# A Mamba-2 mixer's scan: the far outputs transposed back into PSUM first, the own blocks one slot later on top of them

## What is computed

```python
def ssd_chunked(x, dt, a_neg, bm, cm):            # one direction, chunks of 128 tokens
    def step(state, inp):
        cum = jnp.cumsum(ac, axis=1)
        decay = jnp.exp(jnp.where(mask, cum[:, :, None] - cum[:, None, :], -jnp.inf))
        scores = jnp.einsum('btgn,bsgn->btsg', cc, bc)
        y_intra = jnp.einsum('btsg,btsgr,bsgr,bsgrp->btgrp', scores, decay, dtc, xc)
        y_state = jnp.einsum('btgn,bgrpn,btgr->btgrp', cc, state, jnp.exp(cum))
        ...
        return state, y_intra + y_state

def mamba2_bidir_mixer(h, ...):
    proj = h @ w_in                                # gives z, x, B, C and dt
    ...
    y = y_fwd + y_bwd + d_skip[:, None] * xs
    u = (y * silu(z)); u = u * rsqrt(mean(u * u)) * norm_g   # by group
    return u @ w_out
```

## Time and profile before

| | |
|---|---|
| time, median of 3 runs | 2614.88 us (2612.96 to 2616.8) |
| span of the profiled execution | 2614.5 us, the one time that is listed for it |
| PE busy, share of the span | 2547.8 us, 97% |
| DVE busy | 2072.9 us, 79% |
| ACT busy | 1366.4 us, 52% |
| POOL busy | 662.4 us, 25% |
| DMA | 679.73 MB, mean 260 GB/s |
| mixer: first scores of a scan to the last | 1225 to 1860 us of the span |

### The profile page before, as it was taken

The page is one execution under the profiler, slowest core; times in us unless marked ns, Lnnn a source line. Parts: engine busy times, 40 slices in busy tenths (PEclk is TensorE's granted clock), DMA queues, the critical chain, the costliest instruction groups (busy, mean ns, idle before and its releaser), DMA issues.

```text
span 2614.5 us, 45356 instructions
## 1 busy us (share of the span) xinstructions
PE 2547.8 (97%) x15582; PEld 2257.1 (86%) x15582; DVE 2072.9 (79%) x2637; ACT 1366.4 (52%) x2149; POOL 662.4 (25%) x576
## 2 busy tenths in 40 slices
PE   7799999999999999999999999999999999999998
PEld 6799999888888888888788888888888888888887
DVE  7988888898888988758788898888899655555554
ACT  4544444544444444556666646766654444444454
POOL 0011122343444444320011042113333111111123
PEclk8999999999999999999999999999999999999999
DMA  9979988898988989746555598554479555555554
GB/s 395 416 291 368 370 335 304 277 359 306 334 332 328 320 334 326 262 165 204 186 194 194 194 350 286 194 195 160 161 277 336 190 186 188 190 192 184 189 184 142
DMA packets 163918, 679.73 MB, mean 260 GB/s; under 512 B 18720, under 2 KB 18976, under 8 KB 139072
## 3 DMA queue, kind: packets, MB, share of 16 engines
q1 hardware_dynamic: 163728, 677.75, 72.9%
q0 software_dynamic: 48, 0.13, 0.0%
HBM read 675.58 MB, written 2.23 MB: 259 GB/s over the span
## 4 chain that ended last, share of the span: by engine, by line
PE 81%; DVE 9%; issue 3%; DMA 3%; ACT 2%; POOL 0%; DVEq 0%; ACTq 0%; SPq 0%; POOLq 0%
PE psm L1155 43%; PE psm L1158 21%; DVE wl L1484 4%; PE psm L1233 3%; PE psm L1235 3%; PE psm L1234 3%; DVE adat L1497 2%; DMA xs<-in_ada 1%; PE psr L1193 1%; ACT wh L730 1%; PE psm L1449 1%; DVE xs L1497 1%; PE psr L1402 1%; DMA raw<-in_w 1%; PE psr L1449 1%
## 5 line engine op out<-in xcount | busy, mean ns | idle before, releaser
L1484 DVE TENSOR_TENSOR wl<-raw,wh 128x1024 fp32r<-128x1024 f32 x854 | 1109.1, 1300 | 357.4 <-ACT wh L730 354.8
L730 ACT ACTIVATE wh<-raw 128x1024 fp32r<-128x1024 f32 x854 | 897.8, 1053 | 310.1 <-DMA raw<-in_w 138.9
L1155 PE MATMUL psm<-hcat,wh 128*128 128x512 f32 x3120 | 986.6, 398 | 1.4 <-DVE pad L1795 1.4
L1155 PE MATMUL psm<-hid,wh 128*128 128x512 f32 x2240 | 704.6, 396 | 2.3 <-POOL hid L631 2.1
L1158 PEld LDWEIGHTS psm<-hcat,wl 128*128 128x128 f32 x3120 | 586.1, 188 | 138.6
L1158 PE MATMUL psm<-hcat,wl 128*128 128x256 f32 x3120 | 613.3, 278 | 0.0
L1158 PEld LDWEIGHTS psm<-hid,wl 128*128 128x128 f32 x2240 | 420.8, 188 | 99.3
L1155 PEld LDWEIGHTS psm<-hcat,wh 128*128 128x128 f32 x3120 | 476.1, 189 | 7.5 <-issue 5.2
L1497 DVE CUSTOM_DVE_ANT_0 adat<-adat,cond 128x2048 f32<-128x2048 f32 x176 | 434.7, 2470 | 15.8 <-DMA adat<-in_ada 15.7
L1158 PE MATMUL psm<-hid,wl 128*128 128x256 f32 x2240 | 440.1, 278 | 0.0
L1155 PEld LDWEIGHTS psm<-hid,wh 128*128 128x128 f32 x2240 | 341.3, 189 | 3.8 <-POOL hid L631 3.4
(11 more groups left out here) (257 smaller groups left out, 2640.1 us busy)
## 6 DMA issues: line engine op xcount, KB each, us to landing
raw<-in_w SPq DMA_DIRECT2D x866, 512.0 KB, 4.4
adat<-in_ada SPq DMA_DIRECT2D x176, 1024.0 KB, 6.9
dec<-running_sums SPq DMA_DIRECT2D x48, 256.0 KB, 5.9
xs<-in_ada SPq DMA_DIRECT2D x8, 1024.0 KB, 11.4
zs<-in_ada SPq DMA_DIRECT2D x8, 1024.0 KB, 11.6
normt<-running_sums SPq DMA_DIRECT2D x16, 256.0 KB, 4.9
x<-in_xT SPq DMA_DIRECT2D x4, 512.0 KB, 9.5
out<-x SPq DMA_DIRECT2D x4, 512.0 KB, 3.5
```

What stands on the lines that cost most here:

```text
L730: act.activation(wh[:, h % 4, :], raw[:, h % 4, :], ACT.Copy).then_inc(hi_done, 1)
L1155: pe.matmul(both, wh[:, h % 4, (k + i) * P:(k + i + 1) * P], src[:, kb + i, :, :], start=(kb + i == 0), stop=(kb + i == KB - 1), skip_grou ...
L1484: dve.tensor_tensor(wl[:, h % 4, :], raw[:, h % 4, :], wh[:, h % 4, :].bitcast(F32), ALU.subtract).then_inc(lo_done, 1)
```

## The change

On PE the eight products with the identity become eight transposes (`is_transpose`), and they come first: they open the sums in `psr` (`start`), and the own blocks are added on top. So the wait for `y_far` moves from the end of slot 6 to the start of slot 5. The own blocks of pieces 1 and 2 move from slot 4 to slot 5, piece 3 from slot 5 to slot 6; piece 4 stays in slot 6. (Group 0: far outputs and pieces 1 and 2 in slot 6, 3 and 4 in slot 7.) Within a piece the two heads alternate by chunk. The semaphore `y_back` goes; those that waited for it wait for `y_head`. As the pieces' buffers come free later, SP's loads of sums move to slots 5, 5, 6, 6 (group 0's scan: 6, 6, 7, 7), DVE's `segments` to 6, 7, 8, 9 (7, 8, 9, 9), and ACT's `decays` of pieces 1 and 2 to 7 and 8 (8 and 9).

```diff
+def segment_slots(g):
+
+    return {7: (1,), 8: (2,), 9: (3, 4)} if behind(g) else {6: (1,), 7: (2,), 8: (3,), 9: (4,)}
...
-                            if s == (0, 4 + behind(g - 1), 4 + behind(g - 1), 5 + behind(g - 1), 6)[piece]:
+                            if s == (5, 5, 6, 6)[piece - 1] + behind(g - 1):
                                 load_sums(g, piece)
...
-                    at_least(pool, y_back, g + 1)
+                    at_least(pool, y_head, g * HG + HG)
...
-                        for piece in {6: (1,), 7: (2,)}.get(s - behind(g - 1), ()):
+                        for piece in {7: (1,), 8: (2,)}.get(s - behind(g - 1), ()):
                             decays(g, piece)
...
+            def far_back(g):
+
+                at_least(pe, g_ready, g * 4 + 4)
+                at_least(pe, y_far, g * 2 + 4)
+                for b in range(XB):
+                    for ch in range(2):
+                        at = (b % 2) * T + ch * P
+                        pe.matmul(psr[b // 2][:, at:at + P], ytok[:, ch, b * P:(b + 1) * P], ident[:, :],
+                                  start=(b % 2 == 0 and ch == 0), stop=False, is_transpose=True,
+                                  skip_group_check=True)
+
             def own_block(g, piece):
 
                 at_least(pe, em_ready, g * 4 + piece)
                 b = piece - 1
-                for i in range(2):
-                    cols = slice((2 * b + i) * HD, (2 * b + i + 1) * HD)
-                    for ch in range(2):
-                        at = (b % 2) * T + ch * P
+                for ch in range(2):
+                    at = (b % 2) * T + ch * P
+                    for i in range(2):
+                        cols = slice((2 * b + i) * HD, (2 * b + i + 1) * HD)
                         mm = pe.matmul(psr[b // 2][i * HD:(i + 1) * HD, at:at + P], xd[:, 0, ch, cols],
                                        em[piece][:, 2 * ch + i, ch * P:(ch + 1) * P],
-                                       start=(b % 2 == 0 and ch == 0), stop=False,
-                                       skip_group_check=True)
-                    mm.then_inc(y_head, 1)
+                                       start=False, stop=(ch == 1 and b % 2 == 1), skip_group_check=True)
+                        if ch == 1:
+                            mm.then_inc(y_head, 1)
+                return mm
...
-                if s == 4 + behind(g):
-                    at_least(pe, g_ready, g * 4 + 4)
+                if s == 5 + behind(g):
+                    far_back(g)
                     for piece in (1, 2):
                         own_block(g, piece)
-                if s == 5 + behind(g):
-                    own_block(g, 3)
-                if s == 6:
-                    own_block(g, 4)
-                    at_least(pe, y_far, g * 2 + 4)
-                    for b in range(XB):
-                        for ch in range(2):
-                            at = (b % 2) * T + ch * P
-                            mm = pe.matmul(psr[b // 2][:, at:at + P], ytok[:, ch, b * P:(b + 1) * P], ident[:, :],
-                                           start=False, stop=True, skip_group_check=True)
-                    mm.then_inc(y_back, 1)
+                if s == 6 + behind(g):
+                    for piece in (3, 4):
+                        mm = own_block(g, piece)
...
-                    at_least(dve, y_back, g + 2)
+                    at_least(dve, y_head, g * HG + 2 * HG)
...
-                        for piece in {5: (1,), 6: (2,), 7: (3,), 8: (4,)}.get(s - behind(g - 1), ()):
+                        for piece in segment_slots(g - 1).get(s, ()):
                             segments(g, piece)
```

More of the change, by code:

```diff
@@ L314, in build @@
         em_ready, y_head = sem("em_ready"), sem("y_head")
-        y_back, v_done, vz_done, gsq = sem("y_back"), sem("v_done"), sem("vz_done"), sem("gsq")
+        v_done, vz_done, gsq = sem("v_done"), sem("vz_done"), sem("gsq")
         gss, gsum, grms, gu = sem("gss"), sem("gsum"), sem("grms"), sem("gu")
@@ L437, in build @@
         last = At(NG - 1)
-        AHEAD = [(y_head, HG), (y_far, 2), (y_back, 1), (v_done, XB), (grms, 1), (gu, XB), (u_lo, 1)]
+        AHEAD = [(y_head, HG), (y_far, 2), (v_done, XB), (grms, 1), (gu, XB), (u_lo, 1)]
         def first_slot(k):
```

## The result

The changed kernel takes **2662.68 us** (median of 4, 2661.34 to 2665.23) against 2615.73 us for the kernel before in the same sessions: ratio 1.0177, 95% interval 1.0165 to 1.0189. The forecast was 2655 us; it is slower by 47 us where 40 were worked out.

The account below looks back on a forecast made before the run. PE was taken as the bound, without gaps in an ordinary group. Waits 24.2, scan 0 -5.0, shift 9.0 and clock 11.9 sum to 40.1 us on 2614.5, plus 0.4 to the median: 2655 us, range 2632 to 2674.

Parts of the forecast that it names:

- The wait for `y_far`: PE at slot 5 stands for DVE's far product: +3.42 us per ordinary scan, 24.2 us over scans 1 to 7.
- The shift: Moved ACT and DVE steps make `y_far` 1.5 us later in scans 1, 2, 3, 5, 6, 7: 9.0 us.
- the meeting of DVE and POOL: In DVE's slot 9, piece 4 of `segments` brings work to meet POOL's 2.56 us product; 1.5 us charged.
- The clock: PE's granted clock falls behind the new gaps: 1.7 us in each of scans 1 to 7, 11.9 us.
- the wait alone: Rival: PE waits for `y_far` as in the old trace, shift hidden and clock held or recovered: 2634 us, chance 0.12.
- Scans 3 and 7: Scan 3, costed like the ordinary scans, was worked out 6.6 us longer; scan 7, over the output projection's slabs, 7.1.
- Scan 0: First scan gains, as PE's 4.29 us stand for piece 4 goes: -5.0 us, ends -2 and -5.7.
- PE's own cost: PE's scan work in slots 4 to 6 falls from 4.63 to 3.41 us: 1.22 us less per scan without waits.
- The rival of slow transposes: Rival: transposes with open sums take the products' 1.98 us, not 0.87: 8.9 us more, 2664 us, chance 0.07.
- The rival of heads that overlap only when they alternate: Rival: alternating heads halve own-block time once more on PE: 7.7 us less, 2647 us, chance 0.05.
- The other signs: In the new profile, the load of the root's table was to come 1.2 us later against its scan's scores.
- costing the DMAs at nothing: SP's moved loads of sums cost nothing; a late load would show as ACT waiting for `raw`.

Follow-up runs that it names:

- e1: The changed kernel with DVE's scaling of the far outputs (`y_far`) moved to right behind the first `wl` of its slot 3: 2621.61 us, ratio 1.0023.
- e4: The changed order of sums with transposes and all four own pieces in slot 6, the wait one slot later: 2619.2 us, ratio 1.0009.
- e2: The changed kernel with segments of piece 4 back in slot 8 and the exponential of piece 2 in the next group's slot 1: 2652.44 us.
- e3: The changed kernel with unused identity products on PE ahead of the `y_far` wait, 22 in scans 1, 2, 3, 5, 6 and 12 in scan 4: 2652.57 us.
- e7: The changed kernel with far outputs scaled earlier on DVE and the later steps of the decay pieces moved out of the way: 2607.19 us, ratio 0.9969.
- e5: The kernel before, with only its eight identity products made transposes, still last in slot 6 on top of the own blocks: 2609.37 us, ratio 0.9977.
- e6: The kernel before, with only the order within an own block changed, the two heads alternating by chunk: 2615.88 us, ratio 1.0001.
- e9: The kernel before with transposes last, scan 0's piece 4 and far outputs one slot later, own blocks in two visits, not three: 2602.56 us.
- e10: The kernel before with transposes last, scan 0's late steps one slot later, two own-block visits and heads alternating by chunk: 2600.38 us, ratio 0.9938.

## Why the prediction was right

**The wait for `y_far`.** The main step, that PE comes to slot 5 ahead of DVE's far product, held in every scan from 1 to 7 and not in scan 0. From the scores, the transposes start at 38.45 us where slot 5 had begun at 32.72. e1 takes the wait away by moving two DVE instructions, e4 by moving PE's step: both take back over 40 us. That DVE can't be sooner, as I wrote, holds only for its steps in the order as it stands: e1 changes that order, and `y_far` comes 4.6 us sooner.

**The shift.** Foreseen as 1.5 us a scan, measured as 2.14 in scans 2, 3, 5 and 6 and as nothing in scan 1 (38.3 before and after). The step that was mis-sized is the meeting of DVE and POOL: I charged 1.5 us for it, but piece 4 took 2.15 us longer (3.28 against 1.13). In scan 7 it was larger still (below). And the 1.5 us charged in scan 1 did not come at all, since there `y_far` already lay at 38.3 us before the change. The shift also stands behind a cost that I had left out: the gap of 1.57 us ahead of unit 4, which e2 removes in scans 2, 3, 5 and 6. In the changed kernel that gap costs little of its own, as PE would have spent it at slot 5.

**The clock.** 1.7 us a scan was a fair mean, and in part luck: e3 gives 1.9, 1.4, 2.7, 1.4, 2.7, together 10.0 where 8.5 were worked out, and scan 4, where I charged 1.7 for the 2.99 us gap, kept its clock. The rival *the wait alone*, 2634 us, is refuted by e2 and e3 at once: shift and clock cost 10 us each.

**Scans 3 and 7** lost 3.1 and 2.5 us more than worked out. In scan 3, 1.0 is clock, and 1.2 lies in the output units behind it, where PE stands 1.08 us for `wl`. That gap is in the traces of the changed kernel, e1 and e3, and only 0.20 us of it in e2 and e7, which take the later steps of the pieces away; so the moved steps of ACT and DVE bring it, and which of the two is open. The rest, 0.9, is what the other ordinary scans have too: 0.64 of shift and 0.3 of PE's own cost. In scan 7 the step that was mis-sized is the shift: `y_far` comes 34.9 us after the scores (1815.45 us) where it came 31.1 after them, 3.8 us later for the 1.5 charged, 2.3 of the 2.5 us. Timeline of DVE and PE in scan 7:

```profile
1827.14 0.70 PE L1458 MATMUL psr<-hid,wh 128*128 128x512 f32 x2 [1.41 <-issue]
1838.56 0.70 PE L1458 MATMUL psr<-hid,wh 128*128 128x512 f32 x2 [1.10 <-issue]
1849.03 1.28 DVE L1888 TENSOR_TENSOR xd<-psy,normt 128x512 f32<-128x512 f32 x2
1850.46 1.94 PE L1363 MATMUL psr<-ident,xd 128*128 128x128 f32 x8 [6.09 <-DVE xd L1888]
```

In e2 `y_far` is back at 31.1 us there and the two smaller waits are gone, so they come with the later steps too; why the shift is larger in this scan was not taken apart.

**Scan 0** gained 4.7 for 5.0. The own blocks that left slot 5 bought nothing, as foreseen, and a bit less: the gap ahead of unit 5 grew from 0.91 to 1.95 us, and half clock followed it.

**PE's own cost.** 1.22 us a scan were worked out, if nothing waits. e7 shows 0.91 to 0.93 with a wait of 0.24 left, near it, but the parts were not sized right: e5 shows 0.93 for the transposes alone where 1.1 were priced, and e6 0.09 for the order of the heads, put at nothing. The rival of slow transposes is out: the eight take 1.03 to 1.09 us on the timeline at full clock in each of the ten kernels that have them. That is the pace of L1381, whose 0.87 is its share of the chain; on the timeline of before it takes 1.04 us:

```profile
1648.94 1.04 PE L1381 MATMUL psy<-ident,xs 128*128 128x128 f32 x8
```

The two measures differ by what overlaps the row before, so 0.87 against the 1.98 of the products promised a bit too much. At half clock they take 1.88 to 1.97 us, as much as the products at full clock. The Trainium skill, page "TensorE: Matmul & The Clock Gate", section "PE-mode transpose", has some 275 ns for one transpose in a kernel's context; by that figure eight would take 2.2 us (an estimate). The trace agrees for one (270 ns at the least in the changed kernel), and the measured 1.03 to 1.09 us for eight decide against adding it up for transposes in a row. Whether transposes count for the clock was not isolated. The rival of heads that overlap only when they alternate is out by e6. In e9 one visit to the 64-column products less is worth 0.37 us, where the rows had given 0.20 behind the visit and left the part ahead of it open. The Trainium skill, page "TensorEngine Tiling (Array Packing)", section "Key Properties", says that a change of tiling mode drains TensorE; the 0.37 us agree with that, though what makes them up was not taken apart.

**The other signs.** The load of the root's table starts 2.34 us ahead of the scores of scan 5 where it started 3.50 ahead, 1.16 us later, for the 1.2 foreseen. Nothing speaks against costing the DMAs at nothing: between 1225 and 1900 us of the span ACT waits 17.3 us for `raw`, and 34.4 before the change. The whole was worked out 7 us too low: scans 3, 6 and 7 lost 7.5 us more than worked out and scans 2 and 5 1.2, and scans 1 and 4 2.6 less.

## What to carry to other kernels

When a consumer is moved to an earlier slot, compare the time at which it will now arrive with the end of its producer, each measured from the same mark of the period, before counting what the reordering saves. A step that waits belongs on the last slot that its reader allows, and the producer's last step behind nothing that can stand after it: here two instructions of DVE decided some 41 us. Ask, too, whether the saving needs the move at all: e10 has the transposes and one visit less without moving the wait, and is the fastest. Steps that are "only shifted by a slot" on helpers land beside other work; look at what they will meet there (a table load, a product of POOL), not at the helper's mean load.

## What the runs showed of the hardware that was not expected

- The length of a gap did not tell whether PE's clock falls. Behind 1.95 us (scan 0, changed kernel) it ran at 0.55 for 3.5 us, and behind 1.96 us in the same scan of e2 it stayed at 1.00; behind 2.99 us it stayed at 1.00 in scan 4 of the changed kernel and fell to 0.52 in the same scan of e2; behind 5.14 us it was near half for 3.4 us in scan 5 and for the like of 5.8 us in scan 3; by e3 it cost 1.4 to 2.7 us. Filling the gap with products (e3) kept it at 1.00 in scans 1 to 6. The stretches, in this order: scan 5 of e3; scan 0 of the changed kernel, behind its 1.95 us; scan 0 of e2, behind its 1.96 us:

```profile
1702.00:1706.00 4.00, 4.00 (x35) 3.39 (x36) 3.64 (x6) 0.60 (x1) 0.00 (x0) 1.00 0.44 136
...
1260.20:1263.70 3.50, 3.50 (x14) 2.97 (x13) 3.43 (x10) 3.50 (x11) 0.00 (x0) 0.55 0.69 250
...
1258.50:1262.50 4.00, 3.97 (x22) 3.52 (x23) 3.93 (x10) 4.00 (x11) 0.00 (x0) 1.00 0.76 252
```

- DVE's `segments` stood nearly still while POOL's fp32 product ran: 3.28 us for work that takes 1.13 elsewhere, beside 2.48 us of POOL. The same happened to the `wl` of before (2.73 for 1.22, beside 2.56).
- A transpose in fp32 adds onto an open sum in PSUM, with 64-column products in the same bank, at the pace of one that writes: 1.09 us for eight in e5, 1.07 in e1.
